# Output projection and routing in one block, picks ahead of the norm, tables through TensorE, tail rows kept

## The chip, the core and the metric

The kernel runs on one core of a Trainium2 chip. A core has TensorE (PE, matmuls), VectorE (DVE), ScalarE (ACT), GpSimd (POOL) and SyncE (SP, which mostly issues DMAs); each works through its own instructions in order and waits on semaphores for the others. The metric is the device time of one execution in microseconds.

## What is computed

One layer of a decoder trunk, all in float32: 2048 prompt tokens and 8 x 8 sample tokens, 1024 wide. After the mixers each token goes through the output projection, a layer norm, a modulation, and a mixture of 32 experts (4 groups of 8; the best group, and in it the best two experts).

```
mix = jnp.concatenate([y_conv, y_rec], axis=-1) @ w_out
x = _layer_norm(DEEPNORM_ALPHA * x + gate1 * mix, ln_g[0], ln_b[0])
u = x * (1.0 + scale2) + shift2
# routing of u: group by argmax, two experts of the group, softmax weights,
# tokens sorted by expert into blocks of 128 rows
h = jax.nn.silu(xblk @ w_gate[ex]) * (xblk @ w_up[ex])
y_moe = (h @ w_down[ex]) weighted and summed over the token's two experts
x = _layer_norm(DEEPNORM_ALPHA * x + gate2 * y_moe, ln_g[1], ln_b[1])
```

## The kernel before

The program is a row of blocks. Inside a block each engine has its own list of instructions, and a block ends for all engines when the last of them is through. The order of everything is written out by hand; there is no scheduler. After modulation and mixers come four blocks:

**Output stage** (`output_phase`). 17 row tiles t of 128 tokens (the last has 64). SyncE loads y(t) (`load_y`, three slots) and x(t); ScalarE copies y to its upper half `y_hi` (`hi`), VectorE makes the lower half `y_lo` (`lo`), and TensorE forms the product in three passes (hi x hi, hi x lo, lo x hi, `contract`). VectorE's `residual(t)` adds x and takes mean and variance, GpSimd makes `rstd`, VectorE's `norm(t)` writes x1, and GpSimd makes u2 of it in two instructions. TensorE transposes u2 (`transposes`, into `px`) in the middle of the product of tile t+2 and multiplies it by the router weights after that product (`route`, into `pl`); ScalarE moves both (`to_sb`, `keep_logits`). SyncE's list for tile t is `load_y(t+3)`, `load_x(t+2)`, `store(t)`, and `store(t)` waits for x1 and then for u2 of tile t.

**Picks.** The tiles are routed in batches 0-3, 4-7, 8-11, 12-14 and 15-16. In the code a batch is (a, b), from tile a up to but not including tile b. VectorE does `pick_groups` and `pick_first` in its turn for tile t = b+1, `pick_second` at t = b+2, and `place_rows`, which needs TensorE's `count_rows`, at t = b+3. So batch 0-3 falls in turns 5, 6 and 7, batch 4-7 in 9, 10 and 11, and batch 8-11 in 13, 14 and 15. GpSimd then scatters the rows into the list (`scatter_rows`).

**Routing** (`routing_phase`). A block of its own: the end of batch 12-14, batch 15-16, and then VectorE's table of blocks (which expert, which place in the list). The table goes from `tab_i` to memory and back into `blk_tab` by two DMAs of SyncE, which stand behind the loads of the first three experts' weights. ScalarE and VectorE split the weights of experts 0 and 1 into halves (`split_high`, `split_low`).

**Experts** (`expert_phase`). For each block of 128 rows: GpSimd fetches the ids and gathers the rows; TensorE transposes them, multiplies by gate and up weights in three passes and by the down weights; GpSimd scatters the result to y2. SyncE keeps loading weights, three slots each.

**Last stage** (`combine_phase`). 17 tiles: load y2 and x1, sum, layer norm, store.

## Time and profile before

| | us |
|---|---|
| median of 3 runs | 1959.36 |
| lowest, highest | 1959.23, 1959.64 |
| the profiled execution | 1958.05 |
| its span | 1956.5 |
| TensorE busy in the span | 1760.3 (90%) |
| VectorE busy | 1143.1 (58%) |
| ScalarE, GpSimd busy | 616.6, 597.1 |

The trace is of one execution. All positions are microseconds from the start of the span; durations come from the instruction records. A row of the time line gives start, duration, engine, line, operation, output and input, and in brackets how long the engine had been idle and what ended that.

### The profile page before, as it was taken

Reading aid. Unit: us, or ns where it says so; the run is one execution under the profiler, and the core shown is the slowest. Engines: PE = TensorE matmul, PEld = TensorE weight load, DVE = VectorE, ACT = ScalarE, POOL = GpSimd, SP = SyncE. Lnnn points to the kernel's source line nnn. Section 1 sums busy time; section 2 is a strip of 40 time slices with the busy share of each in tenths; the row PEclk is TensorE's granted clock in tenths of the full one; section 3 lists DMA queues with packets and bytes.
Section 4 is the critical chain, followed back from the end, with each engine's and each line's share of the span. In section 5 each row is a group of like instructions: output and inputs, shape, how many; then the busy total and the mean of one; then the engine's idle time right before and its main releaser. Section 6 shows DMA issues by size and latency. Waiting matters only on the chain. (4 is left out here: it accounts for less than half of the span.)

```text
span 1956.5 us, 29481 instructions
## 1 busy us (share of the span) xinstructions
PE 1760.3 (90%) x9152; PEld 1374.9 (70%) x9153; DVE 1143.1 (58%) x1864; ACT 616.6 (32%) x770; POOL 597.1 (31%) x685
## 2 busy tenths in 40 slices
PE   5999999999999999999689989139999999999674
PEld 3888878888888899999478777127666777666331
DVE  4566665556666766565467778714456333455198
ACT  3333332222333222222211110205465434455142
POOL 0122222111222222102145556413444333344155
PEclk8999999999999999999799989569999999999897
DMA  8444334443333232331664342558899864798495
GB/s 262 140 141 131 115 99 139 131 133 111 98 99 91 87 87 59 90 108 41 218 187 151 130 130 98 166 176 275 282 358 339 310 231 167 252 315 301 194 387 182
DMA packets 302076, 342.76 MB, mean 175 GB/s; under 512 B 19077, under 2 KB 257446, under 8 KB 299537
## 3 DMA queue, kind: packets, MB, share of 16 engines
q1 hardware_dynamic: 278872, 284.30, 45.3%
q0 software_dynamic: 18000, 55.87, 7.9%
q10 hardware_dynamic: 5106, 1.31, 0.4%
q8 instruction: 57, 0.93, 0.2%
q14 instruction: 41, 0.34, 0.1%
HBM read 276.86 MB, written 64.58 MB: 175 GB/s over the span
## 5 line engine op out<-in xcount | busy, mean ns | idle before, releaser
L1534 DVE TENSOR_TENSOR w_gu_lo<-w_gu_raw,w_gu_hi (+1 forms) x64 | 146.4, 2291 | 158.3 <-ACT w_gu_hi L1527 158.2
L896 DVE TENSOR_TENSOR w_lo<-w_raw,w_hi 128x1024 fp32r<-128x1024 f32 x112 | 138.1, 1236 | 139.4 <-ACT w_hi L546 136.7
L658 POOL TENSOR_TENSOR o_r<-o_ms,neg_half 128x4 f32<-128x4 f32 (+1 forms) x16 | 16.8, 1051 | 663.0 <-DVEq L932 663.0
L1907 PE MATMUL ph<-w_gu_hi,x_hi 128*128 (+1 forms) x408 | 178.6, 438 | 12.9 <-DVE hh L1869 10.4
L713 PE MATMUL pr<-ub_hi,w_hi 128*128 128x288 f32 (+1 forms) x672 | 189.2, 335 | 0.0
L713 PE MATMUL pr<-ub_hi,w_lo 128*128 128x288 f32 (+1 forms) x672 | 184.2, 328 | 0.0
L713 PE MATMUL pr<-ub_lo,w_hi 128*128 128x288 f32 (+1 forms) x672 | 183.6, 327 | 0.0
L713 PE MATMUL pr<-ua_hi,w_hi 128*128 128x512 f32 x448 | 182.6, 408 | 0.0
L1935 PE MATMUL py<-w_dn_w,hhT 128*128 x400 | 180.9, 595 | 0.8 <-ACT hhT L1839 0.4
L713 PE MATMUL pr<-ua_hi,w_lo 128*128 128x512 f32 x448 | 177.0, 395 | 0.0
L713 PE MATMUL pr<-ua_lo,w_hi 128*128 128x512 f32 x448 | 176.9, 395 | 0.0
L1907 PE MATMUL ph<-w_gu_hi,x_lo 128*128 (+1 forms) x408 | 160.4, 393 | 0.0
L1907 PE MATMUL ph<-w_gu_lo,x_hi 128*128 (+1 forms) x408 | 160.1, 392 | 0.0
L1862 DVE TENSOR_TENSOR x_lo<-pxe,x_hi 128x1024 f32 (+1 forms) x52 | 63.5, 1220 | 142.6 <-ACT x_hi L1831 142.6
L546 ACT ACTIVATE w_hi<-w_raw 128x1024 fp32r<-128x1024 f32 x112 | 117.9, 1054 | 51.7 <-PE pr L713 42.5
L1527 ACT ACTIVATE w_gu_hi<-w_gu_raw (+1 forms) x64 | 122.1, 1911 | 31.0 <-DMA w_gu_raw<-in_w_e_up 13.6
L1935 PEld LDWEIGHTS py<-w_dn_w,hhT 128*128 128x128 f32 x400 | 74.7, 189 | 79.6 <-issue 76.7
L713 PEld LDWEIGHTS pr<-ub_hi,w_hi 128*128 128x128 f32 x672 | 113.3, 188 | 18.0 <-issue 9.0
L713 PEld LDWEIGHTS pr<-ub_hi,w_lo 128*128 128x128 f32 x672 | 113.4, 188 | 10.2
L713 PEld LDWEIGHTS pr<-ub_lo,w_hi 128*128 128x128 f32 x672 | 113.7, 188 | 8.7
L670 POOL TENSOR_TENSOR kl<-kl,wl 128x256 f32<-128x256 f32 (+1 forms) x112 | 89.1, 796 | 93.2 <-DVEq L1035 76.1
L1907 PEld LDWEIGHTS ph<-w_gu_hi,x_hi 128*128 128x128 f32 x408 | 77.2, 189 | 48.3 <-issue 35.4
(334 smaller groups left out, 3482.5 us busy)
## 6 DMA issues: line engine op xcount, KB each, us to landing
w_raw<-in_w_in SPq DMA_DIRECT2D x112, 512.0 KB, 4.2
w_gu_raw<-in_w_e_gate SPq DMA_DIRECT2D x32, 1024.0 KB, 8.3
w_gu_raw<-in_w_e_up SPq DMA_DIRECT2D x32, 1024.0 KB, 11.9
w_dn_w<-in_w_e_down SPq DMA_DIRECT2D x32, 1024.0 KB, 10.1
w_mod<-in_w_mod SPq DMA_DIRECT2D x16, 1024.0 KB
y_t<-y_scratch SPq DMA_DIRECT2D x16, 1024.0 KB, 7.1
w_ring<-in_w_mod SPq DMA_DIRECT2D x4, 2048.0 KB, 17.4
x_cols<-in_x_prompt SPq DMA_DIRECT2D x32, 256.0 KB, 5.5
```

Of the source, the lines that this page charges most:

```text
L546: act.activation(w_hi[:, n % WS], w_raw[:, n % WRAW], ACT.Copy).then_inc(hi_done, 1)
L658: pool.tensor_tensor(o_r[:, 0:c], o_ms[:, 0:c], keep["neg_half"][:, 0:c], ALU.pow).then_inc(o_rs, 1)
L670: pool.tensor_tensor(dst[:, :, 0, :], src[:, :, 0, :], wr, ALU.mult)
L713: last = pe.matmul(pr[n % 2][:, a * 512:a * 512 + c], w[:, n % WS, k, :], x[:, k, a * c:(a + 1) * c], start=(k == 0 and m == 0), stop=(k = ...
L896: dve.tensor_tensor(w_lo[:, n % WS], w_raw[:, n % WRAW], w_hi[:, n % WS].bitcast(F32), ALU.subtract).then_inc(lo_done, 1)
L1527: act.activation(w_slot(keep["gu_hi"], s, lo, hi), w_slot(keep["gu_raw"], r, lo, hi), ACT.Copy).then_inc(keep["gu_h"], 1)
L1534: dve.tensor_tensor(w_slot(keep["gu_lo"], s, lo, hi), w_slot(keep["gu_raw"], r, lo, hi), w_slot(keep["gu_hi"], s, lo, hi).bitcast(F32), AL ...
L1862: dve.tensor_tensor(x_lo[:, bass.ds(half, 1), :].rearrange("p a w -> p (a w)"), px[:, :], x_hi[:, bass.ds(half, 1), :].rearrange("p a w -> ...
L1907: last = pe.matmul(ph[:, :], x[:, half, k * P:(k + 1) * P], w_slot(w, s, k * GU, (k + 1) * GU), start=(k == 0 and m == 0), stop=(k == KT - ...
L1935: last = pe.matmul(py[:, hf * 512:(hf + 1) * 512], hhT[:, k, :], w_slot(dn_w, s_down, at, at + 512), start=(k == 0), stop=(k == KD - 1))
```

## The change

**One block.** `routing_phase` is gone; its work stands at the end of the lists of `output_phase`, with batches 12-14 and 15-16 as the fourth and fifth of five batches. The scratch arrays of the output stage (`wo_raw`, `wo_hi`, `wo_lo`, and `z`, `z2`, `x1`, `u2T`) now lie in the buffers of the expert weights (`gu_raw`, `gu_hi`, `gu_lo`). The gate and up weights of expert 0 are loaded at tile 8, those of experts 1 and 2 after the last routing matmul; the first three down weights at the start of the expert block.

**Order in a tile.** VectorE does `residual`, `lo(t+3)`, the picks, and then `norm`. ScalarE does `hi(t+2)` before `to_sb(t-2)`. The picks of batch 12-14 come after the last tile. u2 of the last tile is made by VectorE (`modulate_last`) and no longer by GpSimd.

**Table.** Two TensorE matmuls by the identity turn `tab_f` into one row, and VectorE copies it to `blk_tab`; the two DMAs are gone. `blk_tab` is laid out as all experts, then all places.

**Tail.** During the last experts SyncE loads the gate, the norm rows and x1 of the first eight tiles into `gu_raw`; `combine_phase` reads them there, and has separate semaphores for y2 and x1.

```diff
@@ output_phase
-    BATCH = ((0, 4), (4, 8), (8, 12), (12, 15))
+    BATCH = ((0, 4), (4, 8), (8, 12), (12, 15), (15, TILES))
-        wo_raw = sb("wo_raw", [P, KT, D])
+        wo_raw, wo_hi, wo_lo = (keep[n][:, 0:2, :].rearrange("p s (k d) -> p (s k) d", d=D) for n in ("gu_raw", "gu_hi", "gu_lo"))
+        mod_s = wo_raw[0:NSAMP, 4:7, :]
+        late = keep["gu_raw"][:, 2, :].rearrange("p (k d) -> p k d", d=D)
+        z, z2, x1 = late[:, 0, :], late[:, 1, :], late[:, 2:4, :]
+        u2T = wo_raw[:, 7, :].rearrange("p (k t) -> p k t", k=KT)
...
                     if t + 2 < T:
                         load_x(t + 2)
+                    if t == 8:
+                        sp.wait_ge(list_out, 16)
+                        load_gate_up(sp, io, keep, 0, 0)
                     store(t)
...
+                sp.wait_ge(lg_ps, T)
+                for e in range(1, RAW):
+                    for landed in ("wg_in", "wu_in"):
+                        sp.wait_ge(keep[landed], 16 * e)
+                    load_gate_up(sp, io, keep, e, e)
...
                 for t in range(2, T):
-                    to_sb(t - 2)
                     if t + 2 < T:
                         hi(t + 2)
+                    to_sb(t - 2)
                     keep_logits(t - 2)
...
+                for e in range(2):
+                    act.wait_ge(keep["wg_in"], 16 * e + 16)
+                    act.wait_ge(keep["wu_in"], 16 * e + 16)
+                    for a in range(2):
+                        split_high(act, keep, e, a, e, e)
...
+                for i in (3, 4):
+                    pe.wait_ge(mm_rdy, i + 1)
+                    count_rows(pe, keep, rk, *BATCH[i], rk_rdy)
+                pe.wait_ge(tab_rdy, 1)
+                for c in range(2):
+                    last = pe.matmul(rk[0:1, c * P:(c + 1) * P], tab_f[:, c:c + 1], ident[:, :], start=True, stop=True)
+                last.then_inc(tab_ps, 1)
...
+                def modulate_last():
+                    n, s = rows_of(LAST), LAST % 2
+                    dve.wait_ge(u2_rdy, LAST)
+                    dve.wait_ge(u2_out[s], 16 * (LAST // 2))
+                    dve.wait_ge(uT_ps, LAST - 1)
+                    dve.wait_ge(scale_s_rdy, 1)
+                    dve.drain()
+                    dve.tensor_tensor(u2[0:n, s, :], x1[0:n, s, :], mod_s[0:n, 2, :], ALU.mult)
+                    dve.drain()
+                    dve.tensor_tensor(u2[0:n, s, :], u2[0:n, s, :], mod_s[0:n, 1, :], ALU.add).then_inc(u2_rdy, 1)
+
                 for t in range(T):
                     residual(t)
-                    norm(t)
                     if t + 3 < T:
                         lo(t + 3)
-                    dve.drain()
...
-                    for i, (a, b) in enumerate(BATCH):
-                        if t == b + 1:
+                    for i, (a, b) in enumerate(BATCH[0:4]):
+                        if t == b + 1 and t < LAST:
                             dve.wait_ge(lg_sb, b)
                             pick_groups(dve, R, a, b, gd_rdy)
                             pick_first(dve, R, a, b)
...
                         if t == b + 3:
                             place_rows(dve, R, rk, a, b, gs_rdy, w_rdy, rk_rdy, i, dest_rdy)
+                    norm(t)
+                    dve.drain()
...
+                modulate_last()
                 a, b = BATCH[3]
+                dve.wait_ge(lg_sb, b)
+                pick_groups(dve, R, a, b, gd_rdy)
+                pick_first(dve, R, a, b)
                 pick_second(dve, R, a, b, dm_rdy, mm_rdy)
@@ end of the tables
-                dve.tensor_copy(tab_i[:, :], tab_f[:, :])
                 dve.drain().then_inc(tab_rdy, 1)
+                dve.wait_ge(tab_ps, 1)
+                dve.tensor_copy(blk_tab[:, :], rk[0:1, 0:2 * P])
+                dve.drain()
                 for e in range(2):
                     for a in range(2):
                         split_low(dve, keep, e, a, e, e)
@@ expert_phase
+                for e in range(RAW):
+                    if e:
+                        sp.wait_ge(wd_in, 16 * e)
+                    load_down(sp, io, keep, e, e)
                 sp.wait_ge(xg_in, 32)
                 gate_up(3, 0)
...
+                for t in range(EARLY):
+                    tail(NE - 2 + t // 4, t % 4, P, scr["x1"][t * P:(t + 1) * P, :])
+                sp.wait_ge(tail_in, 16 * (3 + DEC_B + EARLY))
@@ combine_phase
+                    sp.dma_start(y2[0:n, s, :, :], scr["y2"][t * 2 * P:t * 2 * P + 2 * n, :].rearrange("(p k) d -> p k d", k=2)).then_inc(y_in[s], 16)
+                    if t >= EARLY:
+                        s = (t - EARLY) % R
+                        if t >= EARLY + R:
+                            sp.wait_ge(xa_rdy, t - R + 1)
+                        sp.dma_start(x1[0:n, s, :], scr["x1"][t * P:t * P + n, :]).then_inc(x_in[s], 16)
```

How VectorE's instructions of one tile stood before, in the output stage (L1450 to L1460 are `residual`, L1464 and L1470 `norm`, whose output `x` is x1, and L1438 is `lo`):

```order
L1450 TENSOR_TENSOR z<-pm,mod_p 128x1024 [waits prod2]
L1453 SCALAR_TENSOR_TENSOR z<-x_t,z 128x1024 [waits x2_in1]
L1456 BN_STATS stats<-z 128x6 x2
L1458 BN_AGGR mv<-stats 128x2
L1460 TENSOR_SCALAR ve<-mv 128x1
L1464 SCALAR_TENSOR_TENSOR z<-z,mv,ln 128x1024
L1470 SCALAR_TENSOR_TENSOR x<-z,rstd,ln 128x1024 [waits rs_rdy]
L1438 TENSOR_TENSOR y_lo<-y_raw,y_hi 128x1024 [waits y_h]
```

and how they stand now (L1491 to L1501 `residual`, L1479 `lo`, L1505 and L1511 `norm`; z and x1 lie in `w_gu_raw`, and both appear by that name):

```order
L1491 TENSOR_TENSOR w_gu_raw<-pm,mod_p 128x1024 [waits prod2]
L1494 SCALAR_TENSOR_TENSOR w_gu_raw<-x_t,w_gu_raw 128x1024 [waits x2_in1]
L1497 BN_STATS stats<-w_gu_raw 128x6 x2
L1499 BN_AGGR mv<-stats 128x2
L1501 TENSOR_SCALAR ve<-mv 128x1
L1479 TENSOR_TENSOR y_lo<-y_raw,y_hi 128x1024 [waits y_h]
L1505 SCALAR_TENSOR_TENSOR w_gu_raw<-w_gu_raw,mv,ln 128x1024
L1511 SCALAR_TENSOR_TENSOR w_gu_raw<-w_gu_raw,rstd,ln 128x1024 [waits rs_rdy]
```

`lo`, with its wait for ScalarE's `y_h`, moved from behind `norm` to ahead of it.

SyncE's instructions ahead of the boundary to the experts (L1745), in the routing block, before:

```order
L1540 DMA w_dn_w<-in_w_e_down 128x2x1024
L1516 DMA w_gu_raw<-in_w_e_gate 128x8x256 [waits wd_in,wu_in,wg_in]
L1516 DMA w_gu_raw<-in_w_e_up 128x8x256
L1540 DMA w_dn_w<-in_w_e_down 128x2x1024
L1581 DMA gate_p<-mod_scratch 128x1024
L1583 DMA gate_s<-mod_scratch 8x1024 x8
L1586 DMA tab_scratch<-tab_i 128x2 [waits tab_rdy]
L1588 DMA blk_tab<-tab_scratch 1x256 [waits tab_out]
L1572 UNCONDITIONAL_BRANCH [waits g2_in,tab_in]
L1745 UNCONDITIONAL_BRANCH [waits barrier_Pool_Activation_PE_DVE_SP_release]
```

and now, from the last store of u2 (L1240) over that boundary (L1721), in the joined block:

```order
L1240 DMA u_scratch<-u 64x1024 [waits u2_rdy]
L1628 DMA w_gu_raw<-in_w_e_gate 128x8x256 [waits lg_ps,u2_out1,wg_in,x1_out1,wu_in,u2_out0,x1_out0]
L1628 DMA w_gu_raw<-in_w_e_up 128x8x256
L1628 DMA w_gu_raw<-in_w_e_gate 128x8x256 [waits wu_in,wg_in]
L1628 DMA w_gu_raw<-in_w_e_up 128x8x256
L1217 UNCONDITIONAL_BRANCH
L1721 UNCONDITIONAL_BRANCH [waits barrier_Pool_Activation_PE_DVE_SP_release]
L1652 DMA w_dn_w<-in_w_e_down 128x2x1024
L1652 DMA w_dn_w<-in_w_e_down 128x2x1024 [waits wd_in] x2
L1628 DMA w_gu_raw<-in_w_e_gate 128x8x256 [waits xg_in,gu_l,wg_in,wu_in]
```

The boundary between output and routing, the down weights and both table DMAs (L1586, L1588) are gone from this stretch; the down weights stand behind the boundary to the experts.

## Rows read from the trace of the kernel before

**Rows 1.** Busy time by stage, output and expert stage; us, counts, clock, DMA share, GB/s

```profile
945.00:1222.00 277.00, 243.52 (x1187) 199.94 (x1186) 197.77 (x276) 46.67 (x68) 133.06 (x83) 0.91 0.49 158
...
1304.00:1837.00 533.00, 515.63 (x2132) 357.09 (x2132) 236.49 (x213) 249.99 (x262) 207.43 (x255) 1.00 0.79 272
```

**Rows 2.** Time line of PE: start, duration, what it did; routing, count, first expert matmul

```profile
1201.02 1.87 PE L1401 MATMUL pl<-w_rt,u2T 128*128 128x36 f32 x16
1206.96 0.79 PE L2207 MATMUL rk<-mm,tri 128*128 128x128 f32 x2 [4.08 <-DVEq L2201]
...
1221.33 1.87 PE L1401 MATMUL pl<-w_rt,u2T 128*128 128x36 f32 x16
...
1303.89 0.76 PE L1907 MATMUL ph<-w_gu_hi,x_hi 128*128 128x512 f32 x1 [2.46 <-DVE x_lo L1862]
```

**Rows 3.** Time line of POOL: the first id fetch of the experts

```profile
1290.22 0.59 POOL L1776 DMA_DIRECT2D ids_ring<-list_scratch  x1 [26.70 <-issue]
```

**Rows 4.** Time line of SP: loads of y(5) and y(7), and of the table

```profile
1012.63 0.43 SPq L1214 DMA_DIRECT2D y_raw<-y_scratch  x1
...
1037.43 0.44 SPq L1214 DMA_DIRECT2D y_raw<-y_scratch  x1
...
1284.95 0.21 SPq L1588 DMA_DIRECT2D blk_tab<-tab_scratch  x1
```

**Rows 5.** The tile y_raw: its 17 loads, issue to landing

```profile
DMA to landing us min/median/max: 4.0/4.8/18.3
```

**Rows 6.** Time line of DVE, tile 4: end of residual, x1

```profile
1039.88 0.15 DVE L1460 TENSOR_SCALAR ve<-mv 128x1 f32<-128x1 f32 x1
...
1041.74 1.28 DVE L1470 SCALAR_TENSOR_TENSOR x<-z,rstd,ln 128x1024 f32<-128x1024 f32 x1 [0.51 <-POOL rstd L1344]
```

**Rows 7.** Time line of POOL: u2 of tile 3, its two instructions

```profile
1031.20 3.31 POOL L1355 TENSOR_TENSOR u<-x,mod_p 128x1024 f32<-128x1024 f32 x1 [1.46 <-DVE x L1470]
1034.65 2.39 POOL L1357 TENSOR_TENSOR u<-u,mod_p 128x1024 f32<-128x1024 f32 x1
```

**Rows 8.** Time line of ACT: hi of tiles 3 and 5

```profile
990.48 1.06 ACT L1270 ACTIVATE y_hi<-y_raw 128x1024 fp32r<-128x1024 f32 x1 [0.38 <-DMA y_raw<-y_scratch]
...
1021.26 1.06 ACT L1270 ACTIVATE y_hi<-y_raw 128x1024 fp32r<-128x1024 f32 x1 [5.59 <-DMA y_raw<-y_scratch]
```

**Rows 9.** Time line of DVE: picks of batch 0 (first part) and its placing

```profile
1059.43 0.17 DVE L2151 TENSOR_REDUCE gmax<-logits 128x4 f32<-128x16 f32 x1
1059.67 1.95 DVE L2153 TENSOR_TENSOR gd<-logits,gmax 128x16 f32<-128x16 f32 x1
...
1065.53 0.29 DVE L2189 SCALAR_TENSOR_TENSOR lem<-oh,lem 128x128 f32<-128x128 f32 x1
...
1094.69 0.97 DVE L2228 TENSOR_TENSOR base<-base,rk 128x32 f32<-128x32 f32 x4
...
1098.78 0.16 DVE L2249 TENSOR_TENSOR rows<-psel,w 128x4 f32<-128x4 f32 x1
```

**Rows 10.** DMA issues, page part 6: count, KB each, median us to landing

```profile
ids_ring<-list_scratch POOLq DMA_DIRECT2D x55, 2.0 KB, 5.6
...
y_raw<-y_scratch SPq DMA_DIRECT2D x1, 256.0 KB, 4.0
```

**Rows 11.** Time line of DVE: last x1, picks of 15 and 16, tables, splits

```profile
1228.81 1.28 DVE L1470 SCALAR_TENSOR_TENSOR x<-z,rstd,ln 64x1024 f32<-64x1024 f32 x1 [1.54 <-POOL rstd L1344]
...
1247.48 0.16 DVE L2151 TENSOR_REDUCE gmax<-logits 128x2 f32<-128x8 f32 x1
...
1253.46 0.22 DVE L2199 TENSOR_TENSOR mm<-tmp,valid 128x64 f32<-128x64 f32 x1
...
1258.69 0.19 DVE L1631 TENSOR_TENSOR cnt<-base,ecap 128x32 f32<-128x32 f32 x1
...
1264.80 8.89 DVE L1534 TENSOR_TENSOR w_gu_lo<-w_gu_raw,w_gu_hi 128x2048 fp32r<-128x2048 f32 x4
```

**Rows 12.** Waits of the last stage: who waited for whom, total, times, longest

```profile
PE ps_y L2064 <- DMA x_t<-x_scratch: 16.3, 1, 16.3
```

More of the change, by code:

```diff
@@ L50 @@
 RAW = 3
+EARLY = 8
 MC = 256
@@ L1177, in output_phase @@
         rstd = sb("rstd", [P, 1])
+        cnt = sb("cnt", [P, NE])
+        cnt_i = sb("cnt_i", [P, NE], I32)
+        nb_i = sb("nb_i", [P, NE], I32)
+        nb = sb("nb", [P, NE])
+        cum = sb("cum", [P, 2, NE])
+        cmp_, cmp2 = sb("cmp_", [P, NE]), sb("cmp2", [P, NE])
+        eg, gst = sb("eg", [P, 1]), sb("gst", [P, 1])
+        odd = sb("odd", [1, 1], I32)
+        tab_f = sb("tab_f", [P, 2])
         NLIST = (NE + 1) * CAP // P
-        slot_i = wo_raw[:, 6, 0:NLIST].bitcast(I32)
-        fill = wo_raw[:, 3:6, :].rearrange("p k d -> p (k d)")[:, 0:4 * NLIST].bitcast(I32).rearrange("p (s c) -> p s c", c=4)
+        slot_i = wo_raw[:, 3, 0:NLIST].bitcast(I32)
+        fill = wo_raw[:, 0:3, :].rearrange("p k d -> p (k d)")[:, 0:4 * NLIST].bitcast(I32).rearrange("p (s c) -> p s c", c=4)
         pm = [ps("pm0", [P, 1024]), ps("pm1", [P, 1024])]
@@ L1310, in _ @@
                             pair_shares(act, R, a, b, w_rdy)
-                for t in range(T - 2, T):
-                    to_sb(t)
-                    keep_logits(t)
+                to_sb(LAST - 1)
+                keep_logits(LAST - 1)
+                act.wait_ge(gd_rdy, 4)
+                group_shares(act, R, *BATCH[3], gs_rdy)
+                to_sb(LAST)
+                keep_logits(LAST)
+                act.wait_ge(dm_rdy, 4)
+                pair_shares(act, R, *BATCH[3], w_rdy)
+                act.wait_ge(gd_rdy, 5)
+                group_shares(act, R, *BATCH[4], gs_rdy)
+                act.wait_ge(dm_rdy, 5)
+                pair_shares(act, R, *BATCH[4], w_rdy)
+                for e in range(2):
[3 more added lines that the diff above has]
+                        split_high(act, keep, e, a, e, e)
             @block.gpsimd
@@ L1424, in _ @@
                     route(t - 2)
-                    for i, (a, b) in enumerate(BATCH):
+                    for i, (a, b) in enumerate(BATCH[0:3]):
                         if t == b + 3:
@@ L1431, in _ @@
                     route(t)
+                for i in (3, 4):
+                    pe.wait_ge(mm_rdy, i + 1)
[4 more added lines that the diff above has]
+                last.then_inc(tab_ps, 1)
             @block.vector
@@ L1504, in _ @@
                 a, b = BATCH[3]
+                dve.wait_ge(lg_sb, b)
+                pick_groups(dve, R, a, b, gd_rdy)
+                pick_first(dve, R, a, b)
                 pick_second(dve, R, a, b, dm_rdy, mm_rdy)
[L1508 to L1517 removed]
@@ L1678, in _, with gate_up_w, load_gate_up, w_slot @@
                         split_low(dve, keep, e, a, e, e)
+def gate_up_w(buf, s):
+    return buf[:, bass.ds(s, 1), 0:KT * 2 * DE].rearrange("p a (k c f) -> p (a k) c f", k=KT, c=2)
+def load_gate_up(eng, io, keep, e, s):
+    for c, (w, landed) in enumerate((("w_e_gate", "wg_in"), ("w_e_up", "wu_in"))):
+        eng.dma_start(gate_up_w(keep["gu_raw"], s)[:, :, c, :],
+                      io[w][0, bass.ds(e, 1)].rearrange("e (k p) f -> p (e k) f", p=P)).then_inc(keep[landed], 16)
+def w_slot(buf, s, lo, hi):
+    return buf[:, bass.ds(s, 1), lo:hi].rearrange("p a w -> p (a w)")
+def split_high(act, keep, e, a, s, r):
+    lo, hi = a * KT * DE, (a + 1) * KT * DE
+    act.activation(w_slot(keep["gu_hi"], s, lo, hi), w_slot(keep["gu_raw"], r, lo, hi), ACT.Copy).then_inc(keep["gu_h"], 1)
+def split_low(dve, keep, e, a, s, r):
+    lo, hi = a * KT * DE, (a + 1) * KT * DE
+    dve.wait_ge(keep["gu_h"], 2 * e + (a + 1))
+    dve.tensor_tensor(w_slot(keep["gu_lo"], s, lo, hi), w_slot(keep["gu_raw"], r, lo, hi),
+                      w_slot(keep["gu_hi"], s, lo, hi).bitcast(F32), ALU.subtract).then_inc(keep["gu_l"], 1)
+def load_down(eng, io, keep, e, s):
+    eng.dma_start(keep["dn_w"][:, bass.ds(s, 1), :].rearrange("p a (k n) -> p (a k) n", k=DE // P),
+                  io["w_e_down"][0, bass.ds(e, 1)].rearrange("e (k p) n -> p (e k) n", p=P)).then_inc(keep["wd_in"], 16)
 def expert_phase(nc, io, keep, scr):
@@ L1765, in _ @@
                 down(NE - 1, (NE - 1) % RAW)
+                for i, row in enumerate((scr["mod"][0, 3 * D:4 * D], None, io["ln_g"][0, 1], io["ln_b"][0, 1])):
+                    if row is not None:
+                        tail(NE - 3, i, P, row_bcast(row, P))
+                for b in range(DEC_B):
+                    sp.dma_start(gu_raw[b * DEC_L:(b + 1) * DEC_L, (NE - 3) % RAW, D:2 * D],
+                                 row_bcast(scr["mod"][b + 1, 3 * D:4 * D], DEC_L)).then_inc(tail_in, 16)
+                for t in range(EARLY):
+                    tail(NE - 2 + t // 4, t % 4, P, scr["x1"][t * P:(t + 1) * P, :])
+                sp.wait_ge(tail_in, 16 * (3 + DEC_B + EARLY))
             @block.gpsimd
@@ L1967, in combine_phase @@
         ps_n = ps("ps_n4", [P, D])
-        in_ = [sem("t4_in%d" % s) for s in range(R)]
+        y_in = [sem("y4_in%d" % s) for s in range(R)]
+        x_in = [sem("x4_in%d" % s) for s in range(R)]
         o_out = [sem("o_out%d" % s) for s in range(4)]
```

184 lines of the change are left out of this document (47 added, 137 removed).

## Prediction

> **What bounds the kernel now.** I read the busy time by stage first. In the output stage TensorE works 243.5 of 277 us, which is 14.3 us for each of the 17 row tiles, and in the expert stage 515.6 of 533 us [rows 1]. Both are bound by TensorE, so a later or earlier start of the experts moves the end by as much. I read next where TensorE waits in the output stage: three times for the picks, before the counts of batches 0 to 2, of which the last one, 4.08 us, is shown [rows 2]. Last I read the stretch between TensorE's last row tile, whose product ends where the routing matmul at 1221.3 starts, and the first expert matmul at 1303.9 [rows 2]. It holds the last picks, a block boundary, the table's trip through memory, another boundary and the first gathers.
>
> I call U(t) the moment at which GpSimd has finished u2 of tile t, and E(t) the end of TensorE's product for tile t. E(16) was 1221.3. The first id fetch of the experts was at 1290.2, 68.9 us later [rows 3].
>
> **Part 1, the order inside a tile.** Before, VectorE did residual, norm (which gives x1, from which GpSimd makes u2), then lo(t+3), then the picks. Now lo(t+3) and the picks stand ahead of norm. But lo(t+3) needs hi(t+3), and that needs y(t+3) in place; SyncE's order is unchanged: it issues the load of y(t+3) only after it has stored u2(t-1). So the new order closes a ring: U(t-1), load of y(t+3), hi, lo, picks, norm, U(t). Before, norm did not stand behind lo, and U(t) did not depend on that load.
>
> The trace shows that the load is late. The load of y(7) was issued at 1037.43 [rows 4] and no such load landed in under 4.0 us [rows 5], so it was there after 1041.4; residual(4) was through at 1040.0 and x1(4) was being written from 1041.74 [rows 6]. In the new order x1(4) would have waited for that load, and for hi and lo.
>
> The ring, link by link: u2 done (1034.65 + 2.39 = 1037.04) to issue of the load, 0.4 [rows 4, 7]; issue to landing, median 4.8 [rows 5]; hi 1.1 [rows 8]; lo, as wide as the instructions of norm, 1.3, and two of norm at 1.28 with a drain, 2.7 [rows 6]; x1 to u2 5.9, the 3.31 and 2.39 with their gaps [rows 7]. The sum is **16.2 us per tile**, against 14.3 that TensorE needs. Unsure are the landing (4.0 to about 5.5) and the last link: 5.0 if both GpSimd instructions take the shorter time, 6.7 if both take the longer. VectorE runs residual(t+1) beside them, so I take 5.9. The ring is 14.5 to 17.7.
>
> The picks add to the ring, since they now stand in it. The first part took 6.4 us (1059.43 to 1065.8), less 1.8 by which the second instruction, at 1.95, exceeds its neighbours: 4.6, since GpSimd would rest meanwhile. The second part is eight instructions of 0.36 from start to start, some side by side: 2.7. Placing is 4.4 (1094.69 to 1098.94, and a drain) [rows 9]. In the ring fall three first parts (t = 5, 9, 13), two second parts (6, 10) and two placings (7, 11): 13.8 + 5.4 + 8.8 = 28.0.
>
> Start and end: hi(3) began at 990.48 [rows 8]; with 1.1, 1.3, 2.7 and 5.9 U(0) is 1001.4. Then 13 rounds, 210.6. The load that meets the list's fill took from 1012.63 to 1021.26 until hi began, 3.8 more than 4.8 [rows 4, 8]. The last y is half as wide: 0.8 less to land [rows 10], and about 0.9 less in hi and lo (an estimate from the width). U(13) = 1001.4 + 210.6 + 3.8 + 28.0 - 1.7 = 1242.1. TensorE then has half of tile 15 left (6.9) and tile 16 with routing and count: 1201.02 to 1221.33 less the wait of 4.08, 16.2 [rows 2]. E(16) = 1265.2, **43.9 us later** than 1221.3. That the three waits for picks go is inside this number. Loading expert 0 at t = 8 queues behind y(11): 0 to 3 us, taken as 0.
>
> Here a rule of the Trainium skill would give a shorter ring. By "DMA: Bandwidth & Descriptors", section "Anatomy of one DMA", a transfer costs about 2.0 us and its bytes at 436 GB/s; for 512 KB that is an estimate of 3.2 us. The trace does not agree: 4.0 at least and 4.8 in the median [rows 5]. With 3.2 the ring would be 14.6 and the result 21 us lower.
>
> **Part 2, from E(16) to the first id fetch.** Before, x1(16) ended at 1230.09, 8.8 after E(16) [rows 11]; rstd(16) stands behind scatters again, and I take 8.0. Then all in a row on VectorE: u2 of tile 16 by its own two instructions of 1.28, 2.6; picks of tiles 12 to 14, 6.6 (for two tiles 1247.48 to 1253.7, 6.2); count and placing 5.1 (1253.7 to 1258.69, 5.0); picks, count and placing of 15 and 16, 11.2 (1247.48 to 1258.69); tables 5.8 (1258.69 to 1264.5). That is 39.3. The table's new way is two small matmuls and a read from PSUM; no row has them, the nearest is the count with its hand-overs, 1.2 of the 5.0, and I take 1.8 with the copy (1 to 3). The four lower-half splits took 8.9 [rows 11]; they were hidden under the table's trip, and now nothing covers them, because the block ends only when VectorE is through. Then the boundary: from the issue of the table load at 1284.95 [rows 4] to 1290.2 were 5.3 us, half of it the load, so 2.6 as an estimate. Sum 52.6 in place of 68.9: **-16.3**, ends -12 and -19. ScalarE's upper-half splits and the load of expert 1 lie beside picks and tables. What is saved is the boundary between output and routing and the table's trip, less the splits that it hid.
>
> **Part 3, start of the experts.** The first three w_down loads (3 MB) were done before the expert block; now they are issued at its start, beside the first id fetches and gathers. From the first fetch to the first matmul were 13.7 us with idle queues [rows 2, 3]. An id fetch under load takes 5.6 us to land [rows 10], which is 2 to 3 more than a chain of two fetches and a gather in 13.7 leaves room for, and the gather is exposed alike. I take **+4**, with ends 0 (the queues don't disturb each other) and +10 (TensorE waits for w_down too). Behind that the stage is TensorE's, and keeps its length.
>
> **Part 4, the end.** Eight x1 tiles, the gate and the norm rows are now loaded during the last experts. TensorE's first wait of the last stage is for y2 and x1 together, 16.3 us from the last expert matmul [rows 12]; without x1 (0.5 of 1.5 MB) it ends about 1.3 sooner. VectorE's work there is the same. **-1.3**, ends -5 and 0.
>
> **The sum.** +43.9 - 16.3 + 4.0 - 1.3 = +30.3. The profiled execution (span 1956.5) took 1958.05, so 1988.4; the median of the runs lies 1.3 above it. I predict **1989 us**.
>
> **Rivals.**
>
> A, short ring: loads land near their floor and GpSimd is not held up. The ring is 14.5, 1.7 less in each of 13 rounds: 22 us less, 1967. For it: some load did land in 4.0. Against it: the median, and residual(t+1), which always runs beside u2 now. The skill's rule in Part 1 leads here too.
>
> B, no ring (the other side): y(t+3) is in place before lo wants it. Then picks ahead of norm shorten each of three waits by norm and lo's place, some 3.1 us, -9.3, and with -16.3 + 4 - 1.3 the time is 1936. It decides at one point: the load lands before residual(t) ends. The issue at 1037.43 and the end of residual(4) at 1040.0 speak against it: 512 KB would have to land in 2.6 us.
>
> C, the parts are missized upwards: ring 17.2, and TensorE waits for w_down. 13 + 6 more, 2008.
>
> D, the clock: TensorE now waits in every tile. The granted clock was 0.91 of full over this stage [rows 1]. If it stayed at its lower level of 1.2 GHz through the tiles, TensorE would need twice 14.3 us a tile and bound them in place of the ring: over 2100. The wait of a plain tile is only some 2 us, so it gets little.
>
> E, it nearly cancels: ring at 14.5, gathers undisturbed, small gains at their better ends: 1967 - 4 - 3 = 1960.
>
> **How the numbers follow.** Forecast, ring 15 to 17 (1976 to 2000): 0.54. A: 0.20. C: 0.11. D: 0.02. B: 0.08. E: 0.05, of which 0.03 lies within 0.2% and 0.02 above. 0.2% (3.9 us) is about what a measurement of this kernel can tell from no change. Slower: 0.54 + 0.20 + 0.11 + 0.02 + 0.02 = 0.89; same 0.03; faster 0.08. The range 1963 to 2010 leaves out B, D and E.
>
> **What would show it.** In the changed profile: VectorE is idle some 6 us ahead of y_lo in nearly every tile, released by ScalarE's y_hi, and y_hi by the load of y; the transposes px on TensorE wait for GpSimd's u in most tiles, 1 to 7 us; the routing matmul of tile 14 starts near 1265; the waits before the counts are gone; four splits stand between the table copy and the boundary; the first id fetch is near 1318. The prediction is wrong if y_lo starts right after residual, or if the output stage still ends near 1222.

## The result, and the profile after

The changed kernel takes **1989.95 us** in the median of 4 runs (1988.84 to 1991.54), the kernel before 1959.5 beside it: ratio 1.0156, 95% interval 1.0138 to 1.0174. It is 1.6% slower. The forecast was 1989 in a range of 1963 to 2010. The profiled execution took 1990.14 us with a span of 1988.5, 32.0 more than before.

Read the busy time by stage first, as for the kernel before [rows 1]. The columns are the stretch, its length, busy time and number of instructions of each engine, TensorE's granted clock as a share of full speed, the busy share of the DMA engines and GB/s:

```profile
945.00:1264.00 319.00, 259.88 (x1187) 209.41 (x1187) 181.41 (x278) 46.20 (x68) 114.66 (x81) 0.87 0.44 142
1264.00:1334.00 70.00, 14.25 (x83) 11.93 (x82) 39.70 (x120) 11.65 (x18) 25.76 (x28) 0.54 0.43 133
1334.00:1868.00 534.00, 515.24 (x2132) 357.72 (x2132) 237.35 (x214) 250.58 (x262) 202.75 (x256) 1.00 0.82 282
```

The output stage runs to 1264 and not to 1222. TensorE does the same 1187 matmuls and is idle for 59 of 319 us, where it was idle for 33.5 of 277. The granted clock fell only from 0.91 to 0.87. TensorE's time line gives the marks: routing of tile 14 (where the last product ends), the table's two small matmuls with their start, and the first expert matmul.

```profile
1263.77 1.87 PE L1435 MATMUL pl<-w_rt,w_gu_raw 128*128 128x36 f32 x16
...
1306.86 1.01 PE L1471 MATMUL rk<-ident,tab_f 128*1 128x128 f32 x4 [9.65 <-DVEq L1611]
...
1334.39 0.76 PE L1900 MATMUL ph<-w_gu_hi,x_hi 128*128 128x512 f32 x1 [2.46 <-DVE x_lo L1855]
```

With [rows 2] that is 42.4 us later at the last product and 30.5 at the first expert matmul, so 11.9 were won between the two (70.6 us in place of 82.6).

**The ring.** One turn of it in the time line of all engines (TensorE left out). The last number in brackets is the idle time and who ended it.

```profile
1053.07 0.33 SPq L1240 DMA_DIRECT2D u_scratch<-u  x1
1053.44 0.43 SPq L1224 DMA_DIRECT2D y_raw<-y_scratch  x1
...
1058.34 1.06 ACT L1288 ACTIVATE y_hi<-y_raw 128x1024 fp32r<-128x1024 f32 x1 [9.75 <-DMA y_raw<-y_scratch]
...
1059.43 1.22 DVE L1479 TENSOR_TENSOR y_lo<-y_raw,y_hi 128x1024 fp32r<-128x1024 f32 x1 [6.72 <-ACT y_hi L1288]
1060.57 1.28 DVE L1505 SCALAR_TENSOR_TENSOR w_gu_raw<-w_gu_raw,mv,ln 128x1024 f32<-128x1024 f32 x1
1061.92 1.29 DVE L1511 SCALAR_TENSOR_TENSOR w_gu_raw<-w_gu_raw,rstd,ln 128x1024 f32<-128x1024 f32 x1
...
1063.29 2.40 POOL L1386 TENSOR_TENSOR u<-w_gu_raw,mod_p 128x1024 f32<-128x1024 f32 x1 [9.74 <-DVE w_gu_raw L1511]
...
1065.84 3.17 POOL L1388 TENSOR_TENSOR u<-u,mod_p 128x1024 f32<-128x1024 f32 x1
...
1069.03 0.33 SPq L1240 DMA_DIRECT2D u_scratch<-u  x1
```

Follow it down: u2 of a tile is ready at 1053.07 (its store is issued); the load of y four tiles on (with t the next tile, y(t+3)) follows 0.37 later; `y_hi` starts 4.90 after that, `y_lo` 1.09 later, norm 1.14 later, its second instruction writes x1 from 1061.92 and u2 begins at 1063.29; the next u2 is ready at 1069.03. A turn is **15.96 us**. Five of the thirteen turns from U(0) to U(13) hold neither picks nor the list's fill (GpSimd's DMA into `list_scratch`, at 1018.15) and take 15.9 to 16.2 us. The seven with picks take 140.2 together, and the one that meets the fill takes 19.0.

How often the wait stands there is seen in the waits of 945 to 1280: engine, what it waited for, us in total, times, longest.

```profile
ACT y_hi L1288 <- DMA y_raw<-y_scratch: 191.3, 17, 17.9
POOL u L1386 <- DVE w_gu_raw L1511: 151.3, 16, 15.8
DVE y_lo L1479 <- ACT y_hi L1288: 99.9, 16, 9.8
...
PE px L1424 <- POOL u L1388: 37.9, 10, 9.7
```

So `y_lo` waits in sixteen tiles of seventeen, as the prediction's signs wanted, and the transposes `px` in ten, the longest wait being 9.7 and not 7. Of the waits before the counts of batches 0 to 2, 13.9 us in the kernel before, 1.1 are left.

**The tail.** From the time line after the last product:

```profile
1272.86 0.57 POOL L1375 TENSOR_TENSOR rstd<-ve,neg_half 64x1 f32<-64x1 f32 x1
1273.53 1.34 DVE L1511 SCALAR_TENSOR_TENSOR w_gu_raw<-w_gu_raw,rstd,ln 64x1024 f32<-64x1024 f32 x1 [2.80 <-POOL rstd L1375]
...
1307.90 0.41 DVE L1613 CAST blk_tab<-rk 1x256 int32<-1x256 f32 x1 [1.13 <-PE rk L1471]
1308.39 8.90 DVE L1646 TENSOR_TENSOR w_gu_lo<-w_gu_raw,w_gu_hi 128x2048 fp32r<-128x2048 f32 x4
...
1319.66 0.59 POOL L1769 DMA_DIRECT2D ids_ring<-list_scratch  x1 [13.80 <-issue]
```

The first id fetch is 55.9 after the last product, where it was 68.9 [rows 3]. VectorE's four splits stand alone between the table copy and the boundary. From there to the first expert matmul 14.7 us pass (13.7 before); the expert stage takes 540.0 to the start of the last stage (537.0), and the last stage 114.1 (115.6); its first wait is now for y2 alone [rows 12]:

```profile
PE ps_y L2070 <- DMA y_t<-y_scratch: 14.8, 1, 14.8
```

The balance is +42.4 - 13.0 + 1.0 + 3.0 - 1.5 = +31.9 of the 32.0.

### The profile page after: what moved, and what is told of

Read it like the earlier page. It is cut to its first block and busy times, and to the rows that moved or that the text cites. A ratio compares the mean times of both kernels' runs of the same rounds, so it can differ in the third digit from the quotient of the medians.

```text
span 1988.5 us, 29453 instructions
## 1 busy us (share of the span) xinstructions
PE 1779.7 (89%) x9156; PEld 1386.9 (70%) x9157; DVE 1127.8 (57%) x1866; ACT 616.3 (31%) x770; POOL 571.0 (29%) x683
## 5 line engine op out<-in xcount | busy, mean ns | idle before, releaser
L659 POOL TENSOR_TENSOR o_r<-o_ms,neg_half 128x4 f32<-128x4 f32 (+1 forms) x16 | 16.8, 1050 | 663.1 <-DVEq L933 663.1
L1639 ACT ACTIVATE w_gu_hi<-w_gu_raw (+1 forms) x64 | 121.9, 1909 | 30.8 <-DMA w_gu_raw<-in_w_e_up 14.5
```

The lines of the kernel that those rows point to most:

```text
L1639: act.activation(w_slot(keep["gu_hi"], s, lo, hi), w_slot(keep["gu_raw"], r, lo, hi), ACT.Copy).then_inc(keep["gu_h"], 1)
```

## The experiments

The theory: the new order closes a ring through the load of y, and the picks that stand in it lengthen it; the rest of the change gives time back at the block boundary. The rivals: the picks' or lo's place costs by itself; the merged block and the shared buffers cost; the loads of y are late in any order. The kernel before was run again beside each group: its median was 1959.5 beside the changed kernel, 1958.0 beside e1 to e8, 1957.4 beside e9 and e10, 1956.2 beside e11 and e12. Between medians of different groups 1 to 3 us therefore mean nothing; the ratios compare within a group.

| run | VectorE's order | load of y(t+3) after | last product | median | ratio to before (95%) |
|---|---|---|---|---|---|
| changed | lo, picks, norm | u2(t-1) | 1263.8 | 1989.95 | 1.0156 (1.0138 to 1.0174) |
| e1 | lo, picks, norm | u2(t-2) | 1207.3 | 1928.4 | 0.9851 (0.9835 to 0.9868) |
| e11 | lo, picks, norm | x1(t-1) | 1213.3 | 1934.2 | 0.9880 (0.9863 to 0.9896) |
| e4 | picks, norm, lo | u2(t-1) | 1209.9 | 1932.8 | 0.9871 (0.9852 to 0.9889) |
| e2 | norm, lo, picks | u2(t-1) | 1223.1 | 1945.3 | 0.9945 (0.9926 to 0.9964) |
| e5 | lo, norm, picks | u2(t-1) | 1246.3 | 1962.1 | 1.0023 (1.0011 to 1.0035) |
| before | norm, lo, picks | u2(t-1) | 1221.3 | 1959.5 | |
| e3 | before, lo first | u2(t-1) | 1254.4 | 1990.7 | 1.0163 (1.0146 to 1.0180) |
| e6 | before | u2(t-2) | 1225.1 | 1956.8 | 0.9998 (0.9988 to 1.0009) |

The column "last product" is the start of the routing matmul of tile 14 in the profiled execution. The runs e7 to e10 build on e1 and have their numbers in the text.

**e1: the load one tile earlier.**

```diff
+                load_y(3)
                 sp.wait_ge(wo_l, KT)
...
-                    if t + 3 < T:
-                        load_y(t + 3)
+                    if t + 4 < T:
+                        load_y(t + 4)
```

> The changed kernel, but SyncE issues the load of y(t+4) where it issued that of y(t+3), one tile earlier; the order on VectorE stays lo, picks, norm. Theory T (the ring runs through the load of y): the ring is cut, since the load leaves a whole tile before lo wants it. VectorE's wait before y_lo falls from 6 or 7 us to under 1, TensorE binds the plain tiles again at 14.3 us, the routing matmul of tile 14 starts at 1215 to 1222 instead of 1263.8, and the time is about 1943 us (1936 to 1950). Rival R (the picks and lo ahead of norm cost by their own place on VectorE, the load has little to do with it): plain tiles stay near 16 us and the time stays at 1970 or above.

The ring is gone, and more is won than the theory said (1936 to 1950): 1928.4, 61.6 us less than the changed kernel. VectorE stands before `y_lo` four times, where it stood sixteen: for the three y that are loaded ahead of the tiles and for y(3), and for none behind it:

```profile
DVE y_lo L1480 <- ACT y_hi L1289: 21.4, 4, 9.5
```

The last product came at 1207.3, below the forecast 1215 to 1222, because without the ring the picks ahead of norm are a gain (e4). A plain tile now takes 13.8 us, TensorE's own pace; the 14.3 of the prediction is the mean of all tiles, with counts. The load's place on one queue decides over the sign of the whole change.

**e2: the old order, the rest of the change alone.**

```diff
                     residual(t)
+                    norm(t)
                     if t + 3 < T:
                         lo(t + 3)
...
-                    norm(t)
```

> The changed kernel with VectorE's order inside a tile put back: residual, norm, lo(t+3), picks. Loads of y as in the changed kernel. It holds the other parts of the change alone (one block, table over TensorE, tail rows kept, shared buffers). By the two traces these other parts gave 12.0 between the last product and the first expert matmul, cost 3.0 in the expert stage and gave 1.5 in the last stage: theory T expects 1959.5 - 12.0 + 3.0 - 1.5 = 1949 us (1944 to 1952) and the routing matmul of tile 14 within 2 us of 1221.3. The rival that the longer output stage comes from the merged block or shared buffers and not from the order expects that matmul still after 1240 and a time over 1965.

1945.3 (expected 1949, range 1944 to 1952), and the last product at 1223.1, within 2 us of before. The merged block and the shared buffers don't lengthen the output stage. Together with the table and the tail rows they give 11 to 13 us (by the ratio and by the medians).

**e3: lo first, in the kernel before.**

```diff
                     residual(t)
-                    norm(t)
                     if t + 3 < T:
                         lo(t + 3)
+                    norm(t)
```

> The kernel before with one thing of the change: lo(t+3) stands ahead of norm(t); the picks stay behind norm. Theory T: the ring through the load exists already, at 16 us a plain tile, and without the picks in it: 13 rounds give U(13) near 1211 to 1217 and the last product near 1238, some 17 us later than before, so about 1976 us (1970 to 1984). Rival R (the place of the picks is what costs): within 3 us of 1959.5.

The rival falls: one swapped line costs the kernel before 33 us. The theory had the ring (U in steps of 15.7 to 16.8) but not the whole price; it said 17 and 33.1 came at the last product. Most of the missing 16 stands in TensorE's waits for the picks before the three counts:

```profile
DVE y_lo L1438 <- ACT y_hi L1270: 78.3, 13, 9.8
...
PE rk L2207 <- DVEq L2201: 27.4, 3, 10.1
```

The three waits sum to 27.4 us where the kernel before has 13.9 in three, the last of them 4.08 [rows 2]. My reading, which no run tests by itself: with the ring VectorE reaches the picks later in TensorE's turn, and TensorE stands there before it goes on with the product that VectorE needs next. Two of the rounds took 21.4 and 22.0.

**e4: picks ahead of norm, lo behind it.**

```diff
                     residual(t)
-                    if t + 3 < T:
-                        lo(t + 3)
...
                     norm(t)
+                    if t + 3 < T:
+                        lo(t + 3)
```

> The changed kernel with the picks ahead of norm, but lo(t+3) behind it. Theory T: no ring through the load, since x1 no longer stands behind lo; the picks ahead of norm shorten TensorE's waits for them by the place of norm and lo, some 3 us each, and give back part of it as a later x1. Output stage as long as before or a few us shorter, time 1940 to 1950. Rival R: the picks ahead of norm delay u2 and so the transposes in each tile with picks; the routing matmul of tile 14 comes after 1235 and the time is 1965 or above.

1932.8, better than the theory's range, and 12.4 below e2, which differs from it only in the picks' place. TensorE waits for no count at all before the last product, where e2 has 8.5 us in three. So moving the picks was right, and moving lo with them was not, as long as the load stays where it is: with the load early the same order takes 1928.4 (e1).

**e5: lo ahead of norm, picks behind.**

```diff
                     if t + 3 < T:
                         lo(t + 3)
+                    norm(t)
...
-                    norm(t)
```

> The changed kernel with VectorE's order residual, lo(t+3), norm, picks: the ring through the load of y is closed, but the picks don't stand in it. The order was worth +32.7 us in the kernel before, and the changed kernel in the old order takes 1945.3; theory T (the ring and the picks' place act together: ahead of norm the picks shorten TensorE's waits without the ring, and lengthen the ring with it) expects 1945.3 + 32.7 = 1978 us (1973 to 1983), some 12 us less than the changed kernel. Rival S (the two moves simply add up: picks ahead of norm give 12.4 whatever lo does) expects 1990 + 12.4 = 2002 us.

Neither number: 1962.1. That the two moves don't simply add is clear (2002 would be needed), but my 1978 was wrong too, as it carried over e3's 32.7, of which TensorE's longer waits are a part that this schedule has less of (15.4 us in three). And VectorE's wait is nearly gone in the tiles that follow picks:

```profile
1097.64 0.15 DVE L1501 TENSOR_SCALAR ve<-mv 128x1 f32<-128x1 f32 x1
1097.71 1.22 DVE L1479 TENSOR_TENSOR y_lo<-y_raw,y_hi 128x1024 fp32r<-128x1024 f32 x1
```

Here `y_lo` follows residual at once: the picks of the tile before ran while the load was under way. In the six turns that follow one with picks and still have a `lo`, the wait is 0.6 us at most; in turn 9, which follows one without, it is 3.9, and in the plain turns before the picks 6.6 and 7.0. Behind norm they fill the ring's wait; ahead of it they are added to it. By position in the profiled executions, closing the ring costs 23.3 us at the last product (e2 to e5), and putting the picks into it another 17.5 (e5 to the changed kernel). The medians say 16.8 and 27.9; the runs of e5 spread over 1959 to 1967, so the split between the two is known to some 6 us each way, their sum (41 at the last product, 45 in the medians, 41 with e12's median) better.

**e6: the load one tile earlier, in the kernel before.** The same edit as e1.

> The kernel before with the load of y one tile earlier and nothing else: a control of the load's effect where lo stands behind norm. Theory T: there is no ring to cut, lo waited for hi only in a few tiles and x1 did not stand behind it, so within 3 us of before, 1958 (1953 to 1961). Rival L (loads of y are late in the kernel before too and hold TensorE up): 10 us or more faster, 1948 or less.

No change, 0.9998. The early load is worth 61.6 us where lo and the picks stand ahead of norm, and nothing where both stand behind. The loads are not late in themselves; the ring makes them so.

**e11: one link taken out.**

```diff
                     sp.dma_start(scr["x1"]...).then_inc(x1_out[t % 2], 16)
+                    if t + 4 < T:
+                        load_y(t + 4)
                     sp.wait_ge(u2_rdy, t + 1)
...
-                    if t + 3 < T:
-                        load_y(t + 3)
+                    if t == 0:
+                        load_y(3)
```

> The changed kernel with its order on VectorE kept, and SyncE's load of y(t+4) issued between the store of x1(t) and the store of u2(t), so after x1(t) where the changed kernel has it after u2(t). This takes one link out of the ring, x1 to u2, 5.9 us. Theory T (the ring is a sum of its links): a plain round would be 16.0 - 5.9, near 10.4 us, below TensorE's 14.3, and a round with picks near 15; the ring then costs next to nothing and the time is 1930 us (1926 to 1937), little above the 1928.4 of the load a whole tile earlier. Rival (what counts is that the load stands behind any step of its own tile, or that transfers crowd each other): rounds of 16 us remain, 1950 or more.

1934.2, inside the range. The load still stands in the chain of its own tile, behind x1, and only the 5.9 us from x1 to u2 are out of the ring: that alone gives back 55.8 of the 61.6 (52.4 against the changed kernel measured beside it, e12). The thirteen turns from U(0) to U(13) take 185.3 us, 14.3 each, where the changed kernel's take 239.3. The ring acts as the sum of its links set against TensorE's pace; once it is shorter, it costs little, some 6 us against e1. VectorE still waits 0.8 to 1.2 us before `y_lo` in six tiles, and 5.2 for y(12), whose load now stands behind those of expert 0's weights.

**e7: early load, and the splits moved.** The four lower-half splits go from the end of VectorE's list in the output block to the start of its list in the expert block.

```diff
-                for e in range(2):
-                    for a in range(2):
-                        split_low(dve, keep, e, a, e, e)
...
+                for e in range(2):
+                    for a in range(2):
+                        split_low(dve, keep, e, a, e, e)
                 x_evac(0, 0)
```

> The changed kernel with the load of y one tile earlier, and the four lower-half splits of experts 0 and 1 moved from the end of VectorE's list in the output block to the start of its list in the expert block, where it waits 15.6 us for the first gather. Part 2 of the prediction: the splits are exposed at their full 8.9 us. Then the time is 1928.4 - 8.9 = 1919.5 us (1918 to 1922). Rival: something else ends almost as late there (GpSimd's last scatter lands about 1 to 2 us after the table copy, or the first product waits for the splits in their new place), and 5 us or less are gained: 1923 or more.

1924.4: 4.0 gained, the rival's side by number, by another cause. The boundary did move by the whole cost, since the first id fetch is 4.2 after the table's matmul and was 12.8 in e1. But from the first fetch to the first expert matmul 18.4 us now pass in place of 14.6. Of these 3.9, 2.0 are GpSimd's copy of the ids, which takes 2.19 where it takes 0.20 in e1, and 1.9 are the gather, from whose issue to the first transpose 5.2 us pass in place of 3.3. GpSimd's time line there:

```profile
1253.30 0.59 POOL L1767 DMA_DIRECT2D ids_ring<-list_scratch  x1 [5.16 <-issue]
1257.43 0.57 POOL L1767 DMA_DIRECT2D ids_ring<-list_scratch  x1 [3.54 <-issue]
1258.00 2.19 POOL L1770 COPY ids_now<-ids_ring 128x4 int32<-128x4 int32 x1
```

**e8: and w_down later.**

```diff
+                sp.wait_ge(xg_in, 32)
                 for e in range(RAW):
...
-                sp.wait_ge(xg_in, 32)
```

> The kernel of the run before, and the first three loads of w_down issued only after the first two gathers have landed. Part 3 of the prediction put +4 on these loads lying beside the id fetches and gathers; the traces show 14.7 us from the first fetch to the first expert matmul against 13.7 before, +1.0. Theory T: that 1.0 comes from the loads and goes here (13.7 again), and the stage gains nothing else: 1 us or less, no difference from the run before within its interval. Rival: the loads cost more than the first gathers show (as the +3.0 of the expert stage in the changed kernel), 3 us or more faster. Other side: the first w_down now comes too late for the first block, and TensorE waits 3 us or more for it.

1923.3 against 1924.4, inside the spread of both. The start shows more than the total: the first expert matmul comes 15.4 after the first fetch instead of 18.4, and TensorE waits for no w_down. So behind the moved splits the loads cost 3.0, not the expected 1.0: the second fetch comes 3.1 after the first in place of 4.1, and the gather's 3.3 are back (3.2). The expected 13.7 were not reached here, since GpSimd is still held up.

**e9: only expert 0's splits stay in front.**

```diff
-                for e in range(2):
-                    for a in range(2):
-                        split_low(dve, keep, e, a, e, e)
+                for a in range(2):
+                    split_low(dve, keep, 0, a, 0, 0)
                 x_evac(0, 0)
+                for a in range(2):
+                    split_low(dve, keep, 1, a, 1, 1)
```

> The kernel with the w_down loads later, and of the four lower-half splits only expert 0's two at the start of VectorE's list; expert 1's two stand behind x_lo of the first block. In the two runs before, GpSimd's copy of the first ids took 2.19 and 1.03 us and the issue of the first gather 1.01 and 2.19, where 0.20 and 1.01 are usual, while a split ran on VectorE beside them. Theory T (a split on VectorE holds GpSimd up): the copy takes 0.2 and the gather's issue 1.0 again, the first transposes come 9.0 to 9.5 us after the first fetch instead of 10.96, and the first expert matmul 1.5 to 2 us sooner; time 1921 to 1922 us, within the interval of the run before. Rival: the copy and the issue stay long, since the cause is the DMA queue or the id fetch, and the first transposes stay at 10.9.

The theory holds in the trace, also in the first transposes, 9.1 after the first fetch in place of 11.0. GpSimd's rows, of e8 and then of e9:

```profile
1256.64 1.03 POOL L1770 COPY ids_now<-ids_ring 128x4 int32<-128x4 int32 x1
1258.53 2.19 POOL L1772 DMA_INDIRECT xg<-u_scratch,ids_now  x1 [0.85 <-DMA ids_ring<-list_scratch]
```

```profile
1258.09 0.20 POOL L1770 COPY ids_now<-ids_ring 128x4 int32<-128x4 int32 x1
1259.14 1.01 POOL L1772 DMA_INDIRECT xg<-u_scratch,ids_now  x1 [0.85 <-POOL ids_now L1770]
```

The first expert matmul comes 13.5 after the first fetch: the 13.7 of the kernel before are reached. From the table's matmul to the first expert matmul 17.7 us pass, where e1 has 27.4: 8.7 less up to the first fetch, 1.0 less behind it. The median, 1919.7, lies in runs from 1915.6 to 1926.5, too wide to say more in the total.

**e10: rstd of the last tile ahead of the scatters.**

```diff
-                            if t == b + (3 if b == 12 else 4) + h:
+                            if t == min(b + 4 + h, LAST):
```

> The kernel of the run before, and GpSimd issues all eight scatters of tiles 8 to 11 only after rstd of the last tile, where four stood ahead of it. In the changed kernel VectorE waits 2.80 us for that rstd, and its residual's second instruction takes 2.37 us. Theory T (the 3.1 us by which x1 of the last tile came later than forecast are this wait): the wait falls to about 0.5 or less, the picks of tiles 12 to 14 start 8.0 to 8.5 us after the last product's end instead of 11 to 11.5 to the end of x1, and the time falls by 2.5 to 3 us, to 1918 or 1919. Rival: the scatters now come later and their last one lands after VectorE is through with the tables, so the boundary eats the gain: no change.

```profile
1215.74 1.33 DVE L1512 SCALAR_TENSOR_TENSOR w_gu_raw<-w_gu_raw,rstd,ln 64x1024 f32<-64x1024 f32 x1 [0.51 <-POOL rstd L1376]
```

The wait fell from 2.79 to 0.51, and from the last product to the table's matmul 40.4 us pass in place of 42.7. The 2.3 are there, but the last product itself came 1.1 later in this execution, and the total, **1919.6 us** (ratio 0.9806, 0.9790 to 0.9823), can't be told from that of e9. So nothing of the gain is lost at the boundary, but no gain in time is shown. My wording of where the picks start mixed two marks: they start 11.2 after the last product, 13.5 in e9, so the 8.0 to 8.5 that it named for them was missed; x1 ends 8.4 after it, 10.7 in e9. It is the best version whose runs lie close together: 2% faster than the kernel before and 3.5% than the changed one.

**e12: the changed kernel again.**

> The changed kernel once more, unaltered, for its expert stage: from the first expert matmul to the start of the last stage it took 540.0 us in the first trace, against 535.3 to 535.9 in the four runs that keep its other parts, and 536.1 to 537.6 in the three of the old form. Theory T (the 3.0 of that stage belong to one execution, through the phase of transfers, and not to the change): 535 to 538 us this time. Rival (they belong to the late start of the stage in the changed kernel): 539 to 541 again. The time is 1988 to 1992 in either case.

1986.6, just below the 1988 to 1992 that I named, and the expert stage took 538.2: between the two sides. TensorE's waits for ScalarE's copy of hhT, the transposed input of the down product, 3.7 us in the first trace, are 2.3 here and absent in e2; the wait of 1.1 for w_down is gone. So 1.8 of the stage varies from one execution to the next, and up to 2.9 over e2's 535.3 stay unexplained; e9, which starts that stage early, took 538.9. What sets this length is open.

## Why the prediction was right

| term | forecast | measured |
|---|---|---|
| plain turn of the ring | 16.2 | 16.0 |
| picks in seven turns | +28.0 | +28.2 (140.2 less 7 x 16.0; see below) |
| last y half as wide | -1.7 | inside the line above |
| turn with the list's fill | 20.0 | 19.0 |
| U(13) | 1242.1 | 1241.5 |
| last product, against before | +43.9 | +42.4 |
| last product to first id fetch | 52.6 (-16.3) | 55.9 (-13.0) |
| first fetch to first expert matmul | +4 | +1.0 |
| expert stage | 0 | +3.0 (+1.2 in e12) |
| last stage | -1.3 | -1.5 |
| span | +30.3 | +32.0 |

**Part 1** was right in mechanism and size, link by link: 0.4, 4.8, 1.1, 1.3, 2.7 and 5.9 were forecast for 0.37, 4.90, 1.09, 1.14, 2.72 and 5.74. e1, e3, e6 and e11 show that the ring is the cause: cutting it, building it into the kernel before, issuing the load early where there is no ring, and shortening the ring by one link all moved the time the way it says. The size that the sum of the links gives was met in the changed kernel and in e11, but not in e3 (17 expected, 33 measured) and e5, where TensorE's waits for the picks come in. That the waits for picks would be inside the number was right too. The +28.2 is the picks and the short last y together. From the start of `y_lo` to U the seven turns are 27.8 us longer than plain ones, in the last of them with a `y_lo` shorter by 0.5, so the picks alone are 28.3. From the load to `y_lo` they are 0.6 longer in sum: six of them take 5.9 to 7.2 where a plain turn takes 6.0, and the last, with half the bytes, takes 4.6. What the prediction did not see is how much the picks' place is worth without a ring: it said 9.3 in rival B, and e4 against e2 gives 12.4 to 13.2.

**Part 2**, term by term: x1 of the last tile ended 11.1 after the product and not 8.0, which is nearly the whole miss of 3.3. The step "rstd(16) stands behind scatters again, and I take 8.0" took less than the row it started from (8.8); in the new order u2 of tile 15 ran to 1266.6, so the scatters began 3.0 behind the last product where they had begun 0.4 behind it, and rstd came at 1272.86, 9.1 behind it and not 6.8. e10 took 2.3 of it away by moving the scatters. The other terms held: the way over TensorE, forecast at 1.8 with no row behind it, took 1.45 from 1306.86 to the copy's end at 1308.31; the splits took 8.90 and lay bare, and the boundary took 2.4. Moving the bare splits behind the boundary as they are gains less than they cost (e7), since they then hold up GpSimd, which the prediction did not have; spread out they are hidden whole (e9).

**Part 3** named the right cause and too high a price: in all seven runs of the new form that load w_down at once and leave the splits in place, first fetch to first matmul is 14.5 to 14.7; in the old form it is 13.4 to 13.7, and with the loads later and the splits out of the way 13.5. So the loads cost 1.0, not 4, as the change has them; between e7 and e8, where the gather is issued 2 us later behind the first fetch, they cost 3.0. The fetch under load was costed by the median of the whole stage (5.6 us [rows 10]), which the first fetch does not see: the second followed it after 4.2 us and, in the old form, after 3.3. That the stage "keeps its length" was missed by 1 to 3 us; why is open.

**Part 4** was right.

The sum came out closer than its terms. The misses are -1.5 in Part 1, +3.3 in Part 2, -3.0 at the first gathers, +3.0 in the expert stage and -0.2 at the end, together +1.7 of the span. That they cancel so far is luck; the mechanism and its largest term, +42.4 of +43.9, are not. By its own sum the forecast would be 1989.7 (1988.4 and 1.3), not 1989.

Of the **rivals**, A (a turn of 14.5) fell with the first trace: the load needed 4.9 to hi. What spoke for it, "some load did land in 4.0", was a misread row: the 4.0 of [rows 5] is the last y, which has 256 KB [rows 10]; among the sixteen loads of 512 KB the fastest took 4.5. The 3.2 us that the prediction works out by the Trainium skill is no test of these loads either: the section "Anatomy of one DMA" gives its formula for the path of GpSimd, and SyncE issues the loads of y. D fell: the granted clock of the output stage was 0.87 in place of 0.91. B came true only when the load was moved, and then gave more than its 1936.

## What to carry to other kernels

Before an operation is put ahead of another in one engine's list, follow what it waits for back through every queue, to see whether it comes round to the operation that it now precedes; if it does, add up the links and compare the sum with the time that the binding engine needs for a tile. Look first at where the transfer is issued: one tile earlier on SyncE's queue turned 1.6% slower into 1.5% faster here. And cost work that fills a wait at nothing only while it stands beside the wait; the same picks, moved into the chain, made its turns longer by all of their 28 us, and the kernel slower by 17.5 (at the last product) to 27.9 us (in the medians) than with the picks behind norm (e5).

## What the runs showed of the hardware

**A split on VectorE holds GpSimd up, also in the issue of a gather.** GpSimd's copy of 128x4 numbers takes 0.20 us alone and took 2.19 (e7) and 1.03 (e8) while VectorE made a lower half of the weights by subtracting the upper half from them, both inputs in SBUF, 2.2 us each; the issue of the gather, 1.01 alone, took 2.19 (e8). In e9, where VectorE rests, both are back, and a later copy that meets the splits of expert 1 takes 1.22. The Trainium skill, "SBUF — State Buffer", section "Who interferes with whom", says that a VectorE instruction with two SBUF inputs contends with a GpSimd instruction that reads SBUF; the copy agrees. The same section infers that such an instruction does not hold up the making of descriptors; e8's 2.19 speaks against that for an indirect gather, whose ids lie in SBUF; whether the reading of the ids or the making of the descriptors was held up, no run here tells apart. The same meeting is in twelve of the thirteen turns of the ring: residual's second instruction on VectorE takes 2.1 to 2.15 us beside GpSimd's u2, and 1.23 where they don't meet. In the changed kernel and then in e1:

```profile
1064.63 2.15 DVE L1494 SCALAR_TENSOR_TENSOR w_gu_raw<-x_t,w_gu_raw 128x1024 f32<-128x1024 f32 x1
```

```profile
1055.72 1.23 DVE L1495 SCALAR_TENSOR_TENSOR w_gu_raw<-x_t,w_gu_raw 128x1024 f32<-128x1024 f32 x1
```

GpSimd's second instruction took 3.17 in the turn shown, in place of 2.40. Both sides pay.

**Runs of one kernel spread by 1.5 to 11 us here,** more than the first comparison showed (e5 from 1959.0 to 1966.9 in ten runs, e9 from 1915.6 to 1926.5 in four), so edits worth 1 to 3 us had to be read from positions in the trace and not from totals.
